# Small gaps between the on-chip buffers of a two-layer transformer kernel

## The chip, the cores and the metric

The kernel runs on one core of one Trainium2 chip. The metric is the device time of one execution, in microseconds (us). Engines are named as in the profile: PE is TensorE's matmul, PEld its weight load (which overlaps the matmul), DVE is VectorE, ACT is ScalarE, POOL is GpSimd, SP is SyncE (it issues DMAs here). SBUF is the on-chip memory that the engines read their operands from; a buffer in it takes the same byte range in each of 128 partitions.

## The reference, cut to what matters

512 frames with 1024 channels each go through two blocks, all in float32.

- Block 1: RMS norm, an input projection into 24 tiles of 128 channels, stick-breaking attention, chunked attention with a relative bias, a short convolution, a grouped norm, an output projection; then a gated feed-forward layer (gate and up with 2816 columns each, and down).
- Block 2: RMS norm, an input projection into 42 tiles, a convolution with 31 taps, sliding-window attention with sinks, three further 1024x1024 projections, and a retrieval layer: `q = h @ w_pq`, scores against 2 x 128 sub-keys per head, the 16 best pairs of 8 heads for each frame, and for these experts (of 16384)

```
a   = gelu(einsum("ced,cd->ce", u_emb[idx], h))
out = einsum("ce,ced->cd", gate * a, v_emb[idx])
```

The kernel computes the retrieval densely: every frame against all 16384 rows of `u_emb`, times a table of gates that is zero for the experts that were not chosen, times all of `v_emb`.

## The kernel before, in words

Activations lie transposed, channels on the partitions and 512 frames along the row, so one tile is 128 x 512 float32 (2048 bytes a partition). A float32 product is made from three products of a rounded type, fp32r: each operand is split into a high part (the value rounded by a copy into an fp32r buffer) and a low part (the value less the high part). `three` (L1040) issues high x high (L1042), low activations x high weights (L1043) and high activations x low weights (L1044), each 128x128 weights against 128x512 activations. That is where the lines L1042 to L1044 come from, whatever the stage is.

The weights come in 218 slots of 128 x 2048 float32 (`w_slots`): 90 for the projections, 64 for the table `u`, 64 for the table `v`. Each slot goes through the same pipeline, in two buffers that alternate: SP loads `raw` (L381, L400) when the low part of the slot two before is made; ACT copies `raw` into `wh` (`high`, L531) when PE is through with that buffer; one of DVE (L1640 in the stages with little DVE work, L2208 in the late ones) and POOL (L457, L512) subtracts into `wl`; PE then runs 48 matmuls on the slot (16 pieces of 128x128 weights, three products each). The high and low activations are `hh` and `hl` in most stages, `hidh` and `hidl` in the down projection, `gah` and `gal` for the table `v`, and views `gh`, `gl`, `qh`, `ql`, `z2r`, `csinr` elsewhere. Waits on semaphores alone order the engines (`w_raw`, `w_hi`, `w_lo` or `uv_lo`, `w_used`).

Beside the slots PE does the small matmuls of attention, norms and scores (L1141 to L1345, L1510), in float32 as it stands, and, between pieces of the table `u`, 1024 small float16 matmuls that make the gate table (L1552). DVE does the 31 taps of the convolution (L1910) and the search for the 16 best (`unit`, L2138 to L2184), which runs while PE works on the first slots of the table `u`; the slots after it need its result (L1567).

The memory: `sb` hands out buffers one behind the other, `esb` as well, in stacks that reuse the same space in different stages. Before `hh` stand `cst` (3584 bytes), `vec` (1556 bytes, which the allocator rounds up to 32 bytes) and a few constants. `hh`, `hl`, `xT`, `raw`, `wh` and `wl` have 16384 bytes each, and the buffers behind them (`tmp`, `sqb`, `lnb`, `z1`, `z2`, `hidh`, `ast`, `gah` ...) mostly multiples of 512 bytes. The addresses that follow from that are, for `hh`, 21664, which is 160 modulo 512, and so 160 modulo 512 for `hl`, `xT`, `raw`, `wh`, `wl`, `tmp`, `z1`, `z2`, `hidh`, `hidl`, `gah`, `gal`, `at`, `qT`, `skT` too; `cst` begins at 128 modulo 512, `kdup` at 352.

Of the kernel before, what the change touches and what calls it, by code (L numbers as in the profile page):

```python
# [15 lines left out]
P = 128  # L16
# [162 lines left out]
def build(nc, ins, out):  # L179
    with ExitStack() as ctx:  # L180
        def sb(name, shape, dt=F32):
            return ctx.enter_context(nc.sbuf_tensor(name, shape, dt))
# [14 lines left out]

        ps = ctx.enter_context(nc.psum_tensor("ps", [P, 8, S], F32))
        hh = sb("hh", [P, KD, S], F32R)
        hl = sb("hl", [P, KD, S], F32R)  # L200


        xT = sb("xT", [P, KD, S])
        raw = sb("raw", [P, 2, 2048])
        wh = sb("wh", [P, 2, 2048], F32R)
        wl = sb("wl", [P, 2, 2048], F32R)

        early = ExitStack()

# [2148 lines left out]
```

## Time and profile before

| | us |
|---|---|
| median of 3 runs | 2661.2 |
| lowest, highest | 2659.51, 2662.67 |
| the profiled execution | 2658.19 |
| its span, first to last instruction | 2656.4 |

| engine | busy us | share of the span |
|---|---|---|
| PE | 2619.3 | 99% |
| PEld | 2116.1 | 80% |
| DVE | 1601.4 | 60% |
| ACT | 1028.5 | 39% |
| POOL | 410.3 | 15% |

The mean granted clock of TensorE is 0.998 of full speed. A matmul's end in the trace is modelled, so the duration of one (some 390 ns) overlaps with the next; the distance from one start to the next is what a matmul costs in a dense row of them.

### The profile page before, as it was taken

Reading aid. Unit: us, or ns where it says so; the run is one execution under the profiler, and the core shown is the slowest. Engines: PE = TensorE matmul, PEld = TensorE weight load, DVE = VectorE, ACT = ScalarE, POOL = GpSimd, SP = SyncE. Lnnn points to the kernel's source line nnn. Section 1 sums busy time; section 2 is a strip of 40 time slices with the busy share of each in tenths; the row PEclk is TensorE's granted clock in tenths of the full one; section 3 lists DMA queues with packets and bytes.
Section 4 is the critical chain, followed back from the end, with each engine's and each line's share of the span. In section 5 each row is a group of like instructions: output and inputs, shape, how many; then the busy total and the mean of one; then the engine's idle time right before and its main releaser. Section 6 shows DMA issues by size and latency. Waiting matters only on the chain.

```text
span 2656.4 us, 33800 instructions
## 1 busy us (share of the span) xinstructions
PE 2619.3 (99%) x12616; PEld 2116.1 (80%) x12616; DVE 1601.4 (60%) x2440; ACT 1028.5 (39%) x1334; POOL 410.3 (15%) x147
## 2 busy tenths in 40 slices
PE   8999999999999999999999999999999999999998
PEld 6767888888876778888888888888888888888886
DVE  4467211213999976579998988888344444444444
ACT  4465322214346763232223455555332222222223
POOL 0001455542010003424444000000000000000000
PEclk9999999999999999999999999999999999999999
DMA  5111222222222222223333365465565555555552
GB/s 184 48 48 69 97 102 97 99 95 95 95 84 76 68 80 96 95 95 145 148 142 143 135 230 192 186 233 201 198 229 189 189 189 191 195 197 195 194 196 95
DMA packets 121737, 374.37 MB, mean 141 GB/s; under 512 B 7553, under 2 KB 73217, under 8 KB 92737
## 3 DMA queue, kind: packets, MB, share of 16 engines
q1 hardware_dynamic: 117968, 333.74, 35.5%
q10 hardware_dynamic: 2016, 35.26, 3.4%
q0 software_dynamic: 1680, 4.46, 0.6%
q8 instruction: 39, 0.64, 0.1%
q14 instruction: 34, 0.27, 0.0%
HBM read 301.86 MB, written 69.21 MB: 140 GB/s over the span
## 4 chain that ended last, share of the span: by engine, by line
PE 83%; DVE 13%; issue 2%; ACT 2%; DMA 0%; DVEq 0%; POOL 0%; POOLq 0%; ACTq 0%
PE ps L1042 26%; PE ps L1044 25%; PE ps L1043 25%; PE ps L1552 2%; DVE cand_t L2179 1%; DVE z L1910 1%; DVE cand_t L2175 1%; DVE sel L2181 1%; DVE wl L1640 1%; DVE topi L2141 1%; DVE topi L2151 1%; DVE sc L2144 1%; DVE sel L2184 1%; DVE bpos L2141 1%; DVE bpos L2151 1%
## 5 line engine op out<-in xcount | busy, mean ns | idle before, releaser
L1042 PE MATMUL ps<-hh,wh 128*128 128x512 f32 x1968 | 783.3, 398 | 9.3 <-DVE wl L1646 8.0
L1044 PE MATMUL ps<-hh,wl 128*128 128x512 f32 x1968 | 768.8, 391 | 0.0
L1043 PE MATMUL ps<-hl,wh 128*128 128x512 f32 x1968 | 767.8, 390 | 0.0
L531 ACT ACTIVATE wh<-raw 128x2048 fp32r<-128x2048 f32 x217 | 414.9, 1912 | 771.2 <-PE ps L1044 769.9
L2208 DVE TENSOR_TENSOR wl<-raw,wh 128x2048 fp32r<-128x2048 f32 x101 | 231.3, 2290 | 432.8 <-ACT wh L531 432.8
L1042 PEld LDWEIGHTS ps<-hh,wh 128*128 128x128 f32 x1968 | 370.2, 188 | 98.9 <-issue 15.6
L1044 PEld LDWEIGHTS ps<-hh,wl 128*128 128x128 f32 x1968 | 370.0, 188 | 79.3
L1043 PEld LDWEIGHTS ps<-hl,wh 128*128 128x128 f32 x1968 | 370.7, 188 | 74.3 <-issue 1.0
L1042 PE MATMUL ps<-gah,wh 128*128 128x512 f32 x1024 | 398.7, 389 | 0.0
L1044 PE MATMUL ps<-gah,wl 128*128 128x512 f32 x1024 | 398.7, 389 | 0.0
L1043 PE MATMUL ps<-gal,wh 128*128 128x512 f32 x1024 | 398.7, 389 | 0.0
L457 POOL TENSOR_TENSOR wl<-raw,wh 128x2048 fp32r<-128x2048 f32 x50 | 230.4, 4608 | 637.4 <-ACT wh L531 637.4
L1043 PEld LDWEIGHTS ps<-gal,wh 128*128 128x128 f32 x1024 | 192.2, 188 | 39.9
L1042 PEld LDWEIGHTS ps<-gah,wh 128*128 128x128 f32 x1024 | 192.2, 188 | 39.9
L1044 PEld LDWEIGHTS ps<-gah,wl 128*128 128x128 f32 x1024 | 192.2, 188 | 39.8
L520 POOL TENSOR_TENSOR pf<-pf,at 128x512 f32<-128x512 f32 x3 | 3.7, 1263 | 1185.0 <-ACT at L1029 1185.0
L1910 DVE SCALAR_TENSOR_TENSOR z<-z,vec 128x511 f32<-128x511 f32 (+14 forms) x240 | 163.4, 733 | 0.0
L512 POOL TENSOR_TENSOR wl<-raw,wh 128x2048 fp32r<-128x2048 f32 x27 | 128.2, 4749 | 183.3 <-ACT wh L531 183.3
L952 ACT ACTIVATE ast<-ps 128x512 f32<-128x512 f32 x64 | 38.2, 598 | 242.4 <-PE ps L1044 242.4
L991 ACT ACTIVATE stage<-ps 128x512 f32<-128x512 f32 x128 | 129.4, 1122 | 0.0
L981 ACT ACTIVATE ast<-ps 128x512 f32<-128x512 f32 x64 | 38.2, 598 | 194.8 <-PE ps L1044 194.8
L1640 DVE TENSOR_TENSOR wl<-raw,wh 128x2048 fp32r<-128x2048 f32 x39 | 89.2, 2288 | 21.4 <-ACT wh L531 21.4
(259 smaller groups left out, 3006.8 us busy)
## 6 DMA issues: line engine op xcount, KB each, us to landing
raw<-in_w_slots SPq DMA_DIRECT2D x217, 1024.0 KB, 4.8
a_spill<-ast SPq DMA_DIRECT2D x64, 512.0 KB, 2.6
gate_table<-stage ACTq DMA_DIRECT2D x8, 4096.0 KB, 13.0
at<-a_spill SPq DMA_DIRECT2D x64, 512.0 KB, 5.8
tt<-gate_table SPq DMA_DIRECT2D x64, 512.0 KB, 6.8
lnb<-z POOLq DMA_DIRECT2D x36, 64.0 KB, 1.9
xT<-in_x SPq DMA_DIRECT2D x4, 512.0 KB, 7.2
bt<-in_rel_tiles POOLq DMA_DIRECT2D x1, 2048.0 KB, 12.2
```

The source lines that it names most:

```text
L457: pool.tensor_tensor(wl[:, b, :], raw[:, b, :], wh[:, b, :].bitcast(F32), ALU.subtract).then_inc(sem("w_lo"), 1)
L512: pool.tensor_tensor(wl[:, b, :], raw[:, b, :], wh[:, b, :].bitcast(F32), ALU.subtract).then_inc(sem("uv_lo"), 1)
L531: act.activation(wh[:, b, :], raw[:, b, :], ACT.Copy).then_inc(sem("w_hi"), 1)
L991: act.activation(stage[:, q % 2, :, c:c + 4].rearrange("p e c -> p c e"), ps[:, 2 * j + a, :].rearrange("p (c e) -> p c e", c=4), ACT.Copy ...
L1042: nc.tensor.matmul(bank, whi, xhi, start=start, stop=False)
L1043: nc.tensor.matmul(bank, whi, xlo, start=False, stop=False)
L1044: return nc.tensor.matmul(bank, wlo, xhi, start=False, stop=stop)
L1552: last = nc.tensor.matmul(ps[:, 2 * r + t // 4, NKEYS * (t % 4):NKEYS * (t % 4) + NKEYS], oh[r][:, 0, t, :], oh[r][:, part, t, :], start=( ...
L1640: dve.tensor_tensor(wl[:, g % 2, :], raw[:, g % 2, :], wh[:, g % 2, :].bitcast(F32), ALU.subtract).then_inc(sem("w_lo"), 1)
L1910: dve.scalar_tensor_tensor(acc[:, back:S], u[:, 0:S - back], w, acc[:, back:S], ALU.mult, ALU.add).then_inc(sem("cv2_y" if m == TAPS else ...
L2141: step(dve.max_index(idx[:, a, 0:8], vals[:, a, 0:8], rows[:, a, :]))
L2208: dve.tensor_tensor(wl[:, b, :], raw[:, b, :], wh[:, b, :].bitcast(F32), ALU.subtract).then_inc(sem("uv_lo"), 1)
```

## The change

Four buffers that nothing reads or writes are put between the others: 32 bytes ahead of `hl`, 64 bytes ahead of `wh`, 160 bytes ahead of `wl`, 160 bytes behind `wl`. No instruction is added, removed or moved; only addresses are different.

```diff
         hh = sb("hh", [P, KD, S], F32R)
+        sb("off_hl", [P, 8])
         hl = sb("hl", [P, KD, S], F32R)
-
-
         xT = sb("xT", [P, KD, S])
         raw = sb("raw", [P, 2, 2048])
+        sb("off_wh", [P, 16])
         wh = sb("wh", [P, 2, 2048], F32R)
+        sb("off_wl", [P, 40])
         wl = sb("wl", [P, 2, 2048], F32R)
+        sb("off_rest", [P, 40])
```

Where the buffers then begin, modulo 512 bytes:

| buffer | before | after |
|---|---|---|
| `hh` | 160 | 160 |
| `hl`, `xT`, `raw` | 160 | 192 |
| `wh` | 160 | 256 |
| `wl` | 160 | 416 |
| `tmp` and all buffers behind it that were at 160 | 160 | 64 |
| `kdup` | 352 | 256 |
| `cst` | 128 | 128 |

The last byte in use moves from 228608 to 229024 of the 229376 in a partition.

## Rows read from the trace of the kernel before

**Rows 1.** The page's part 1: busy us, share of the span, instructions.

```profile
PE 2619.3 (99%) x12616; PEld 2116.1 (80%) x12616; DVE 1601.4 (60%) x2440; ACT 1028.5 (39%) x1334; POOL 410.3 (15%) x147
```

**Rows 2.** The page's part 4: the chain that ended last, by engine.

```profile
PE 83%; DVE 13%; issue 2%; ACT 2%; DMA 0%; DVEq 0%; POOL 0%; POOLq 0%; ACTq 0%
```

**Rows 3.** Windows: us, then busy us of PE, PEld, DVE, ACT, POOL; clock, DMA.

```profile
0.00:66.00 66.00, 58.02 (x241) 44.33 (x241) 29.96 (x40) 31.12 (x49) 1.79 (x6) 1.00 0.50 182
...
666.00:866.00 200.00, 188.63 (x938) 144.11 (x937) 191.20 (x352) 102.97 (x230) 15.78 (x32) 1.00 0.26 85
...
2066.00:2266.00 200.00, 200.00 (x884) 165.62 (x883) 84.70 (x73) 54.36 (x38) 0.00 (x0) 1.00 0.57 191
```

**Rows 4.** Timeline of PE and PEld in the table `v`: start us, us, what.

```profile
2199.94 0.39 PE L1042 MATMUL ps<-gah,wh 128*128 128x512 f32 x1
2199.95 0.19 PEld L1043 LDWEIGHTS ps<-gal,wh 128*128 128x128 f32 x1
2200.17 0.39 PE L1043 MATMUL ps<-gal,wh 128*128 128x512 f32 x1
...
2200.40 0.39 PE L1044 MATMUL ps<-gah,wl 128*128 128x512 f32 x1
...
2200.62 0.39 PE L1042 MATMUL ps<-gah,wh 128*128 128x512 f32 x1
...
2205.38 0.39 PE L1042 MATMUL ps<-gah,wh 128*128 128x512 f32 x1
```

**Rows 5.** DMA issues by tile: count, KB each, median us to landing.

```profile
raw<-in_w_slots SPq DMA_DIRECT2D x217, 1024.0 KB, 4.8
```

**Rows 6.** Timeline of PE: float32 matmuls of 512 columns, two each.

```profile
80.06 1.02 PE L1148 MATMUL ps<-sqb,cst 128*128 128x512 f32 x2
...
84.71 1.02 PE L1157 MATMUL ps<-z 64*128 64x512 f32 x2
```

**Rows 7.** One line's instructions: duration ns min/median/max, L1157 in 84.6:85.5.

```profile
L1157 PE MATMUL ps<-z x3: 483/589/589, 84.4 to 85.1; 64*128 64x512 f32 x2, 64*128 64x384 f32 x1
```

**Rows 8.** Groups by line: count, busy us, mean ns, idle before.

```profile
L1044 PEld LDWEIGHTS ps<-hh,wl 128*128 128x128 f32 x1968 | 370.0, 188 | 79.3
...
L1148 PEld LDWEIGHTS ps<-sqb,cst 128*128 128x128 f32 x32 | 5.2, 190 | 1.0 <-issue 0.6
```

**Rows 9.** Single lines, duration ns min/median/max: the fp32r copies and subtractions.

```profile
L531 ACT ACTIVATE wh<-raw x217: 1893/1912/1925, 15.2 to 2621.7; 128x2048 fp32r<-128x2048 f32 x109
L2208 DVE TENSOR_TENSOR wl<-raw,wh x101: 2281/2292/2294, 1473.9 to 2623.7; 128x2048 fp32r<-128x2048 f32 x101
L2251 DVE TENSOR_TENSOR at<-at,tt x128: 683/685/693, 1933.2 to 2616.8; 128x512 f32<-128x512 f32 x128
L457 POOL TENSOR_TENSOR wl<-raw,wh x50: 4596/4605/4631, 248.8 to 1147.7; 128x2048 fp32r<-128x2048 f32 x50
```

**Rows 10.** Groups by form, DVE in 666:1066: the taps, at 4-byte shifts.

```profile
L1910 DVE SCALAR_TENSOR_TENSOR z<-z,vec 128x511 f32<-128x511 f32 x8 | 5.9, 747 | 0.0
...
L1910 DVE SCALAR_TENSOR_TENSOR z<-z,vec 128x504 f32<-128x504 f32 x8 | 5.6, 743 | 0.0
...
L1910 DVE SCALAR_TENSOR_TENSOR z<-z,vec 128x482 f32<-128x482 f32 x8 | 5.4, 715 | 0.0
```

**Rows 11.** Waits, whole span: us in total, times, longest us.

```profile
ACT wh L531 <- PE ps L1044: 769.9, 103, 9.0
POOL wl L457 <- ACT wh L531: 637.4, 50, 216.2
DVE wl L2208 <- ACT wh L531: 432.8, 68, 9.6
```

**Rows 12.** Waits of PE in 1174:1457, the search for the 16 best.

```profile
PE ps L1567 <- DVE sel L2202: 1.3, 1, 1.3
```

**Rows 13.** Windows, 1174:1457: busy us of PE, PEld, DVE, ACT, POOL; clock, DMA.

```profile
1174.00:1457.00 283.00, 281.71 (x1284) 234.62 (x1284) 255.46 (x869) 83.86 (x90) 114.50 (x24) 1.00 0.37 137
```

**Rows 14.** One line's instructions: the product of the search, beside POOL's subtractions.

```profile
L2179 DVE TENSOR_TENSOR cand_t<-cand_t,topf x16: 1224/1226/5406, 1197.3 to 1447.1; 128x1024 f32<-128x1024 f32 x16
```

**Rows 15.** Timeline: PE where it starts again after a pause.

```profile
1458.44 0.39 PE L1043 MATMUL ps<-hl,wh 128*128 128x512 f32 x1
1458.67 0.39 PE L1044 MATMUL ps<-hh,wl 128*128 128x512 f32 x1
...
1459.59 0.39 PE L1042 MATMUL ps<-hh,wh 128*128 128x512 f32 x1
```

## The prediction

> **What bounds the kernel now.** I read the busy shares first, then the chain of waits, then the windows, then the start times of single matmuls, since a change of addresses can only act through how long single instructions take. PE is busy for 2619.3 of 2656.4 us [rows 1], and the chain that ended last is PE for 83% and DVE for 13% [rows 2]. The windows say where the rest is: the first 66 us have 8 us without PE, the stage of the convolution (666:866) 11.4 us, and the late stages none: 2066:2266 has PE busy for all 200 us [rows 3]. So the reader is to see a kernel whose end moves with the pace of PE over about 2370 us, and with DVE in three short stretches.
>
> The pace: in the table `v` the L1042 matmuls at 2199.94 and 2205.38 are 24 matmuls apart, so one costs 5.44 / 24 = 226.7 ns [rows 4]. The 217 equal loads and one that is split make 218 slots [rows 5], at 48 matmuls each that is 10464 matmuls of this form; 10464 x 226.7 ns = 2372 us, 89% of the span. At full clock (2.4 GHz; the windows show 1.00 [rows 3]) 512 columns at one a cycle would be 213.3 ns, so each matmul has 13.3 ns more than its columns, 139 us in all. This is the only place in the trace with something large that a change of addresses might give back, if those 13.3 ns are two reads of SBUF in each other's way.
>
> **The change, part by part.** Nothing is issued more or less; the counts of instructions, waits, DMAs and bytes stay. Each part is an address.
>
> *PE's two streams (`hh`/`hl` or `gah`/`gal` against `wh`/`wl`).* Before, both begin at 160 modulo 512; after, they are apart by 64 to 352 bytes. Does the pace depend on that? Three readings say no.
> First, the trace has pairs of both sorts. L1157 reads `z1` against `z1`, both at 160; L1148 reads `sqb` (160) against `cst` (128). Two float32 matmuls of 512 columns take 1.02 us with the one and 1.02 us with the other [rows 6]. A single one is drawn 589 ns long [rows 7], so the second starts 430 ns behind the first in both.
> Second, the weight load takes 188 ns where both operands are at 160 and 190 ns where the weights are at 128 [rows 8]. A load that was held up by equal places would be the longer one.
> Third, the streams do not stay in step. In one matmul the activations go over 2048 bytes in some 213 ns and the weights over 512 bytes in 188 ns [rows 4, 8]. Their distance therefore grows by about 1500 bytes during each matmul and passes every place modulo 512 about three times; what a fixed distance of 64 to 352 bytes changes is when a meeting falls, not how many there are. Only if the length of a meeting depended on its moment would the sum change.
> The bounds: below, half of the 430 ns of a float32 matmul of 512 columns, which goes over its columns twice (430 / 2 = 215 ns, the nearest row of a matmul without the extra; rows 6 and 7), so 10464 x (226.7 - 215) = 122 us less. Above, the widest steady pace that the trace has for this form, just after a pause: from 1458.44 to 1459.59 are 5 matmuls, 230 ns each [rows 15], so 10464 x 3.3 ns = 35 us more. I take 0, nearest to the comparison of equal and unequal pairs, which differ by less than the 10 ns that those rows resolve (1% of 1.02 us); in the dense stages the sum is sensitive to less, 1 ns a matmul being 10.5 us, so both ends stay for the rivals.
>
> On this, the Trainium skill has something for each side. "SBUF — State Buffer", section "Who interferes with whom", gives TensorE two independent read ports, one for the moving operand and one for the weight load, and says that only DVE and GpSimd contend, over one port pair. By it the gaps do nothing; the even pace of rows 4, with DVE 42% and ACT 27% busy beside it, agrees, but no row before shows the two ports being independent.
> "TensorE: Matmul & The Clock Gate", section "Back-to-back issue gap", speaks the other way: it has N / 2.4 + 2.5 ns for a warm matmul, 215.8 ns for 512 columns. The 215 ns of half a float32 matmul agree with it, the 226.7 ns of the fp32r form do not, so some 11 ns would be there to be won. As an estimate from that page, all of it won is 10464 x 10.9 = 114 us, a time near 2547 us; that is the first rival below, whose own time is worked out from rows.
>
> *ACT, DVE and POOL on `raw`, `wh`, `wl`.* With all three at one place, the subtraction takes 2292 ns for 2048 elements and the product of `at` and `tt` 685 ns for 512 [rows 9]. The difference is 1607 ns for 1536 elements, 1.046 ns an element, and leaves 149 ns as a fixed part. Within one line nothing scatters: 2281 to 2294 over 101 executions, POOL's 4596 to 4631 over 50, ACT's 1893 to 1925 over 217 [rows 9], although other engines and DMAs come and go beside them. Nor does a shift matter that is not a multiple of 16 bytes: the taps read 511, 504 and 482 columns, that is from 4, 32 and 120 bytes into the row, at 747, 743 and 715 ns [rows 10]; 29 columns for 32 ns is again 1.1 ns a column. Value 0. The price if I am wrong is covered: ACT waits 769.9 us for PE, POOL 637.4 and DVE's L2208 432.8 us for ACT [rows 11]. A slot is 48 x 0.2267 = 10.9 us of PE, and copy plus POOL's subtraction take 1.9 + 4.6 = 6.5 us of it [rows 9], so each could grow by 4 us before PE waits. Bounds: 0 from both sides in these stages.
>
> *DVE in the stages where it leads.* From 1174 to 1457 the search is 255.5 us of DVE in 283 us [rows 13], and PE then waits 1.3 us for its result [rows 12]. So a faster search gives at most 1.3 us, and a slower one costs all that is over. All its buffers move together (160 to 64), so their distances from each other stay. The convolution's taps read and write `z2` alone and shift likewise. I take 0. Bounds: a gain of 1.3 us in the search and none elsewhere; a loss of 1% of 283 us, 3 us, which is what the scatter of single DVE lines (under 1% [rows 9]) allows.
> The search has one thing that depends on moments: the product L2179 takes 1226 ns alone and up to 5406 ns when it meets a POOL subtraction [rows 14]. One meeting more or less is 4.2 us, of which a gain can use only 1.3. Which ones meet follows from the order of the waits, which does not change; I leave 0 and keep +4 in the range.
>
> *DMAs.* `raw` takes 4.8 us to land [rows 5] against the 10.9 us of a slot, and the chain holds 0% of DMA [rows 2]. Value 0, covered by 6 us a slot.
>
> The sum is 0 from every part: the profiled execution of 2658.19 us stays 2658 us. It lies 3.0 us under the median of the runs shown (2661.2), which themselves spread over 3.2 us. As the change is compared with that median, the time I give is 2661.
>
> **The rivals.**
> *A, PE's extra cycles are meetings of the two streams, and the gaps avoid them.* For it: the extra is 32 cycles for 512 bytes of weights, a round number (one for each 16 bytes), float32 matmuls do not have it, and in every dense stage the buffers stand at one place. Against: the three readings above. Won as a whole the pace is 215 ns and the time 2661 - 122 = 2539 us; won by a tenth, 2649 us. It decides from 0.5 ns a matmul (5.3 us) on.
> *B, the other side: the equal places are what keeps the streams apart, and the gaps bring them together.* Place: the same 10464 matmuls. For it: the load of the next weights starts 10 ns after a matmul does [rows 4], at the same place, an order that may be favourable, and the price is paid everywhere, since PE has no slack in the late windows [rows 3]. Against: the same readings. At the 230 ns of rows 15 the time is 2661 + 35 = 2696 us; it decides from 0.5 ns a matmul on.
> *C, a meeting of DVE and POOL more in the search.* 2661 + 4 = 2665 us, still within what can't be told from no change.
> *D, the gaps do not do what they say* (rounded away, or nothing is read from the shifted buffers): the same time as my forecast. Each gap is a multiple of 32 bytes, so the addresses do move.
>
> **How the numbers follow.** A measurement of this kernel can tell about 0.2%, 5.3 us, from no change. My forecast with C and D has 0.79 and gives 2655.9 to 2666.5 us. Rival A has 0.12, most of it on a part of the 122 us, and that is the chance of faster. Rival B has 0.09 and gives slower, most of it under 20 us. The range leaves out about half of A and of B: down to 2650 us (1 ns a matmul), up to 2670 us (0.9 ns a matmul).
>
> **What would show it.** The distance between matmuls in the table `v`, 226.7 ns as in rows 4, decides nearly everything: 215 is A, over 227.2 is B, and anything between is their share. The weight load would keep 188 ns; the lines of rows 9 would keep their medians within 10 ns; PE's wait for the search would stay at 1 to 6 us; 2066:2266 would again have 884 matmuls. I am wrong if the pace differs by over 0.5 ns in any dense stage, or if one line of ACT, DVE or POOL becomes longer by so much that PE waits for `wl`.

## The result, and the profile after

The changed kernel takes 2695.0 us (median of 4 runs, 2693.82 to 2695.26) against 2660.5 us of the kernel before: ratio 1.013, 95% interval 1.0114 to 1.0146. It is slower by 34.5 us; 2661 us was forecast, with 2650 to 2670 as the range, so the time lies 25 us outside it. The profiled execution took 2695.26 us with a span of 2693.5 us, 37.1 us over that of before.

Part 1 of the page of the changed kernel, and the chain that ended last [rows 1, 2]:

```profile
PE 2659.4 (99%) x12616; PEld 2118.1 (79%) x12616; DVE 1597.3 (59%) x2440; ACT 1029.3 (38%) x1334; POOL 411.8 (15%) x147
...
PE 93%; DVE 3%; ACT 2%; issue 1%; DMA 0%; POOL 0%; POOLq 0%; SPq 0%; DVEq 0%; ACTq 0%
```

PE has 40.1 us more, the other engines nothing that matters (DVE 4 us less), with the same counts. The chain has lost most of its DVE: 13% before, 3% now.

The windows [rows 3], with the number of instructions in brackets behind each engine's busy time:

```profile
0.00:66.00 66.00, 58.17 (x239) 44.12 (x240) 29.98 (x40) 30.26 (x46) 1.79 (x6) 1.00 0.49 176
...
2066.00:2266.00 200.00, 200.00 (x875) 164.10 (x874) 84.30 (x73) 53.78 (x38) 0.00 (x0) 1.00 0.56 189
```

The first 66 us are as before. In the table `v` PE is busy for all 200 us in both kernels, at the same clock, and gets through 875 matmuls instead of 884. A full row of 9s in the busy digits can hide a slower PE; the count in the window doesn't.

Timeline of PE in the table `v` [rows 4]; all lines behind the change have numbers higher by 2, so L1044 to L1046 are the old L1042 to L1044:

```profile
2299.96 0.39 PE L1044 MATMUL ps<-gah,wh 128*128 128x512 f32 x1
...
2302.71 0.39 PE L1044 MATMUL ps<-gah,wh 128*128 128x512 f32 x1
```

The two are 12 matmuls apart: 2.75 / 12 = 229 ns, where it was 226.7. Over all 1023 trios of that stage which follow each other the starts give 687 ns a trio (high x high, low x high, high x low: 226, 229 and 232 ns to the next start) against 680. On `hh` and `hl` it is worse: 697.7 ns on average over the 1693 trios without other work between (median 699: 235, 230, 232), against 682.0. That average is a mixture: 1117 of these trios take 698 to 700 ns and 576 take 690 to 695, with the same places. On `hidh`, `qh`, `z2r` and `gh` it is 687 as on `gah`.

That accounts for the change: 15.7 ns x 1968 + 6.7 ns x 1024 + 6.6 ns x 496 = 41 us of PE, of which 37 arrive at the end. Part of the rest was hidden in PE's pauses: idle time of PE in the span is 37.1 us before (2656.4 - 2619.3) and 34.1 us after (2693.5 - 2659.4). PE's wait of 1.3 us for the search [rows 12] is gone: a slower PE is now the later of the two.

The lines of the other engines [rows 9], duration ns min/median/max:

```profile
L533 ACT ACTIVATE wh<-raw x217: 1893/1916/1936, 15.3 to 2658.6; 128x2048 fp32r<-128x2048 f32 x109
L2210 DVE TENSOR_TENSOR wl<-raw,wh x101: 2281/2291/2294, 1495.1 to 2660.6; 128x2048 fp32r<-128x2048 f32 x101
L2253 DVE TENSOR_TENSOR at<-at,tt x128: 681/683/693, 1963.0 to 2653.5; 128x512 f32<-128x512 f32 x128
L459 POOL TENSOR_TENSOR wl<-raw,wh x50: 4578/4614/4656, 250.9 to 1163.2; 128x2048 fp32r<-128x2048 f32 x50
```

Medians moved by 4, -1, -2 and 9 ns, 0.3% at most, though `raw`, `wh`, `wl` and `at` now stand at four places instead of one. Only PE minds.

### The profile page after: what moved, and what is told of

Its sections match the earlier page's. It is cut to its first block, busy times and chain, and to the rows that moved or that the text cites. A ratio compares the mean times of both kernels' runs of the same rounds, so it can differ in the third digit from the quotient of the medians.

```text
span 2693.5 us, 33800 instructions
## 1 busy us (share of the span) xinstructions
PE 2659.4 (99%) x12616; PEld 2118.1 (79%) x12616; DVE 1597.3 (59%) x2440; ACT 1029.3 (38%) x1334; POOL 411.8 (15%) x147
## 4 chain that ended last, share of the span: by engine, by line
PE 93%; DVE 3%; ACT 2%; issue 1%; DMA 0%; POOL 0%; POOLq 0%; SPq 0%; DVEq 0%; ACTq 0%
PE ps L1044 29%; PE ps L1046 29%; PE ps L1045 28%; PE ps L1554 2%; DVE z L1912 1%; DVE wl L1642 1%; PE ps L1150 0%; PE ps L1512 0%; PE ps L1218 0%; ACT wh L533 0%; PE ps L1323 0%; PE ps L1229 0%; PE ps L1347 0%; PE ps L1334 0%; PE ps L1245 0%
## 5 line engine op out<-in xcount | busy, mean ns | idle before, releaser
L1044 PE MATMUL ps<-hh,wh 128*128 128x512 f32 x1968 | 798.1, 406 | 8.5 <-DVE wl L1648 7.7
L1046 PE MATMUL ps<-hh,wl 128*128 128x512 f32 x1968 | 778.8, 396 | 0.0
L2210 DVE TENSOR_TENSOR wl<-raw,wh 128x2048 fp32r<-128x2048 f32 x101 | 231.2, 2289 | 440.5 <-ACT wh L533 440.5
L1044 PEld LDWEIGHTS ps<-hh,wh 128*128 128x128 f32 x1968 | 370.2, 188 | 103.2 <-issue 15.6
L1046 PEld LDWEIGHTS ps<-hh,wl 128*128 128x128 f32 x1968 | 370.4, 188 | 92.5
L1046 PE MATMUL ps<-gah,wl 128*128 128x512 f32 x1024 | 403.5, 394 | 0.0
L1044 PE MATMUL ps<-gah,wh 128*128 128x512 f32 x1024 | 397.3, 388 | 0.0
L1044 PEld LDWEIGHTS ps<-gah,wh 128*128 128x128 f32 x1024 | 192.2, 188 | 43.0
L1046 PEld LDWEIGHTS ps<-gah,wl 128*128 128x128 f32 x1024 | 192.5, 188 | 38.2
L2224 DVE TENSOR_TENSOR same<-iota_t,slot_t 128x1024 f16<-128x1024 f16 x64 | 78.2, 1221 | 46.4 <-PE ps L1554 46.3
```

The source lines that it names most:

```text
L1044: nc.tensor.matmul(bank, whi, xhi, start=start, stop=False)
L1046: return nc.tensor.matmul(bank, wlo, xhi, start=False, stop=stop)
L2210: dve.tensor_tensor(wl[:, b, :], raw[:, b, :], wh[:, b, :].bitcast(F32), ALU.subtract).then_inc(sem("uv_lo"), 1)
L2224: dve.tensor_tensor(same[:, :, :], iota_rows, slots(0), ALU.is_equal).then_inc(sem("oh_part"), 1)
```

## The experiments

A single run of an unchanged kernel scatters over some 5 us (the kernel before, in all runs here: 2658.2 to 2662.8), so times are given beside the run of the kernel before on the same chip, and the verdicts rest on the distances between matmuls. "Distance" is the place of the weights less that of the activations, modulo 256 bytes.

### PE alone, one distance at a time (m1_pairs)

```diff
+SETTINGS += [(0, 16 * i) for i in range(64)]
+for n, (m, w) in enumerate(SETTINGS):
+    for r in range(24):
+        nc.tensor.matmul(ps[:, n % 8, :], wt[:, w // 4:w // 4 + P], mv[:, m // 4:m // 4 + S], ...)
```

> Leaves out the whole computation: one fp32r weight tile and one activation row are loaded, and PE alone runs rows of 24 matmuls of 128x512, each row with its own distance between the bytes of the activations and of the weights; nothing else runs beside. Theory S (streams): the cost of an fp32r matmul depends on the distance, modulo 512 bytes or a part of it, between the activations that it reads and the weights that are loaded meanwhile; 226.7 ns at distance 0, as in the kernel before, and values from 216 to 235 ns elsewhere, with period 512. Theory N (neighbours): the pace is lost to reads and writes of DVE, ACT, POOL or DMAs beside PE; then all distances show one pace, at or under 226.7 ns. Theory A (address): it hangs on where a single operand begins; then rows in which both are shifted alike differ from distance 0.

Timeline of PE; each row is 25 matmuls, from the first start to the last end, so (time - 0.39) / 24 is the pace. The rows are distances 0, 32, 96, 192 and 256:

```profile
16.78 5.83 PE L64 MATMUL ps<-mv,wt 128*128 128x512 f32 x25
...
33.10 5.99 PE L64 MATMUL ps<-mv,wt 128*128 128x512 f32 x25
...
55.45 6.00 PE L64 MATMUL ps<-mv,wt 128*128 128x512 f32 x25
...
88.97 5.89 PE L64 MATMUL ps<-mv,wt 128*128 128x512 f32 x25
...
111.12 5.83 PE L64 MATMUL ps<-mv,wt 128*128 128x512 f32 x25
```

The paces from the starts alone, in ns:

```
distance      0     16     32     48     64     80     96    112    128    144    160    176    192    208    224    240
pace      226.7  226.7  233.4  233.3  233.2  232.1  234.3  233.3  233.5  233.5  233.1  230.0  228.9  233.3  233.4  226.8
```

The same 16 values came back over 1024 bytes, within 0.2 ns, and with 96 bytes plus each whole kilobyte up to 6. With activations moved instead of weights the values are those of the negative distance within 0.8 ns. So Theory S holds, but for its period, which is 256 bytes and not 512, and for its lower end: nothing is under 226.7. With nothing beside PE, Theory N falls. Rows with both shifted alike average 226.9 to 227.8 ns, but the excess is in the first seven intervals of a row (224 to 236 ns), where the addresses have just changed; from there on they have 226.7 ns like the rest. So an address by itself is worth nothing here, and what ran before is felt for some matmuls.

### The same in the full kernel (e_shift_all, e_w256b, e_w96b)

```diff
+        sb("off_all", [P, 24])     # e_shift_all: all distances stay 0
         hh = sb("hh", [P, KD, S], F32R)
...
+        sb("off_wh", [P, 64])      # e_w256b: 256 bytes, nothing else
+        sb("off_wh", [P, 24])      # e_w96b: 96 bytes, and 160 behind wl
         wh = sb("wh", [P, 2, 2048], F32R)
```

> The kernel before with one gap of 96 bytes ahead of hh: all buffers of the dense stages begin at 256 modulo 512 instead of 160, their distances from each other stay 0. Theory S: no change, 2660 us, three matmuls in 680 ns. Theory A (an operand at 160 is well placed, one at 256 or 64 is not): slower, between 2665 and 2700 us.

> The kernel before with one gap of 256 bytes ahead of wh: raw and the activations hh, hl at 160 modulo 512, wh, wl and all behind at 416. Theory S with a period of 256 bytes, as in the rows of matmuls: no change, 2658 to 2664 us, three matmuls in 680 ns. With a period of 512 in the full kernel, or if any gap between them costs: the stages on hh slower, over 2675 us.

> The kernel before with one gap of 96 bytes ahead of wh and one of 160 behind wl: wh and wl 96 bytes past the activations modulo 256 in every stage, all the rest at equal places modulo 256. The row of matmuls at distance 96 took 234.3 ns each against 226.7 at distance 0. Theory S: three matmuls in about 700 ns instead of 680, 3488 trios, 60 to 80 us more, about 2720 to 2740 us: worse than the changed kernel, though the gaps are smaller. Theory M (it is having many different distances, not one, that costs): less than the changed kernel's loss, under 2695 us.

| | us | before, same chip | trio on `hh`, ns | trio on `gah`, ns |
|---|---|---|---|---|
| e_shift_all | 2662.7 | 2661.5 | 682.0 | 680.0 |
| e_w256b | 2663.2 | 2659.9 | 682.0 | 680.0 |
| e_w96b | 2726.6 | 2659.9 | 702.9 | 702.9 |

The window 266:466 (on `hh`) of the kernel before, then the windows 266:466 and 2066:2266 (on `gah`) of the kernel with a distance of 96 bytes everywhere:

```profile
266.00:466.00 200.00, 200.00 (x882) 165.25 (x881) 44.00 (x61) 59.95 (x63) 102.93 (x34) 1.00 0.27 97
...
266.00:466.00 200.00, 200.00 (x854) 160.48 (x853) 45.29 (x62) 59.05 (x61) 97.23 (x33) 1.00 0.27 95
2066.00:2266.00 200.00, 200.00 (x855) 160.80 (x854) 80.92 (x70) 51.51 (x36) 0.00 (x0) 1.00 0.55 188
```

3 x 234.3 = 702.9 ns from the row of matmuls is the trio in the full kernel to the tenth. A distance of 96 bytes in every stage costs 67 us, nearly twice the change itself; a gap of 256 bytes, larger than any of the change, costs nothing that can be measured (3 us, 0.13%). Theories A and M fall, and with them a period of 512 bytes.

The profile shows where even the 3 us arise. In e_shift_all and e_w256b the window 666:866, the stage of the convolution, has a granted clock of 0.97 and 914 matmuls, where the profiled kernel before has 1.00 and 938; in 866:2466 they have 7923 and 7922 against its 7919. Both have a mean granted clock of 0.996, as have the runs of the kernel before that took 2661.5 and 2662.8 us; with 0.998 it took 2658.2 and 2659.9. So a difference of 2 to 5 us between single runs can be the clock and not the addresses.

### Is it the buffers behind wl? (e_rest_back, e_rest160)

```diff
-        sb("off_rest", [P, 40])
+        sb("off_rest", [P, 64])    # e_rest_back, from the changed kernel
...
+        sb("off_rest", [P, 40])    # e_rest160, from the kernel before, the only gap
```

> The changed kernel with the last gap 96 bytes larger, so that all buffers behind wl stand at 160 modulo 512 again; hh 160, hl 192, wh 256, wl 416 as in the changed kernel. Theory S: the stages on gah, hidh, qh, z2r and gh now have nearly the distances of hh (96 and 256), and their three matmuls go from 687 to about 694 to 698 ns; 1520 trios by 8 to 11 ns are 12 to 17 us more, 2707 to 2712 us; the stages on hh keep 697 ns. Theory R (the place of the buffers behind wl, for DVE and ACT, costs the time): back towards 2660 us. Theory A: gah and the others at 160 return to 680 ns, 2684 us.

> Only the last gap: tmp and all behind it 160 bytes further; hh, hl, xT, raw, wh, wl at equal places. Map theory: the stages on hh keep 680 ns; in the 1520 others (gah, hidh, qh, z2r, gh) the weights are 96 past the activations modulo 256, (0, 96, 96) is 702.8 ns; 22.8 x 1520 = 35 us, about 2694 us. Part theory, or DVE and ACT being the ones that lose: another pattern, with ACT's or DVE's medians longer by over 1%, or under 2672 us.

e_rest_back: 2699.2 us (before 2661.5); trios 697.4 ns on `hh`, 690.0 on `gah`. Putting those buffers back where they had been made it 3 to 4 us slower still (37.7 us over the kernel before, where the change has 34.5), since `gah` at 160 is now 96 from `wh`; Theories R and A fall. The 690 is less than the 694 to 698 expected, and the time 2699 less than 2707. e_rest160, the windows as above:

```profile
266.00:466.00 200.00, 200.00 (x880) 164.93 (x879) 44.27 (x61) 59.20 (x62) 102.89 (x34) 1.00 0.27 98
2066.00:2266.00 200.00, 200.00 (x855) 160.78 (x854) 82.39 (x72) 49.17 (x35) 0.00 (x0) 1.00 0.56 189
```

880 in the first window against 882 before, 855 against 884 in the second: the loss sits in just the stages whose activations were moved, 702.9 ns a trio. 2696.3 us (before 2662.8) against the 2694 expected.

### The other gaps one by one (e_hl32, e_wh64, e_wl160)

```diff
+        sb("off_hl", [P, 8])       # e_hl32; 224 bytes behind hl bring the rest back
         hl = sb("hl", [P, KD, S], F32R)
...
+        sb("off_wh", [P, 16])      # e_wh64; 192 bytes behind wh
+        sb("off_wl", [P, 40])      # e_wl160; 96 bytes behind wl
```

> Only the first gap: hl 32 bytes further, all the rest at equal places modulo 256. Map theory: the trio map of PE alone has 696 ns for (low activations 32, weights 0, 0) against 680, on the 1968 trios of hh and hl; 16 ns x 1968 = 31 us, about 2690 us, and 680 ns in the table v. Part theory (each gap gives its share of the 34.5 us of the whole change): a third of it or less, under 2672 us.

> Only the second gap: wh 64 bytes further, all the rest at equal places modulo 256. Map theory: (0, 64, 0) is 700 ns against 680, on all 3488 trios; 20 ns x 3488 = 70 us, less some 5 that DVE hides, about 2725 us, twice the loss of the whole change. Part theory: under 2695 us.

> Only the third gap: wl 160 bytes further, all the rest at equal places modulo 256. Map theory: (0, 0, 160) is 700 ns, about 2725 us as with wh alone. Part theory: under 2695 us.

| only this gap | us (before 2662.8) | trio on `hh`, ns | trio on `gah`, ns |
|---|---|---|---|
| hl by 32 | 2684.4 | 697.5 | 680.0 |
| wh by 64 | 2704.6 | 696.8 | 693.3 |
| wl by 160 | 2719.3 | 700.0 | 700.0 |
| rest by 160 | 2696.3 | 681.8 | 702.9 |

The losses are 21.5, 41.8, 56.4 and 33.5 us, 153 us together, for a change that costs 34.5 with all four. (The run of before beside them had a mean granted clock of 0.996, like the last of the four; the others had 0.997, 0.998 and 0.998, so by the runs of before at either clock their losses may be some 2 to 5 us too small.) So the gaps have no shares of their own: what counts is the set of distances that they leave. The map's 696 and 700 ns for hl and wl come back in the kernel (697.5; 700.0), the 700 for wh does not: 697 and 693, and 2705 us instead of 2725. On `hidh`, where the places differ by the same 64 bytes as on `gah`, the same run has 700.0 ns: three paces for one set of distances. For hl the time is 6 us under the one expected although the trio is as mapped: PE is busy for 30 us more than in the profile of before (2649.5 us), but its span is only 26 us longer (2682.6 us), so 4 us went into PE's pauses, and the run of before beside it was 2 us above the one that the expectation started from.

### Which type, which size (m2b_kinds)

```diff
+SETTINGS += [("r", 512, 128, d), ("f", 512, 128, d), ("h", 512, 128, d)]   # fp32r, float32, float16
+SETTINGS += [("r", 448, 128, d), ("r", 384, 128, d), ("r", 512, 96, d), ("r", 512, 64, d), ("r", 512, 32, d)]
```

> Leaves out the whole computation: rows of 24 matmuls of PE alone, of three types (fp32r, float32, float16), at distances 0, 96, 192 and 32 bytes, and fp32r with fewer columns of activations or of weights. Theory S2: only fp32r, which reads 4 bytes a column at one column a cycle, has no room for the reads of the weights, so float32 (about 430 ns) and float16 (about 216 ns) show the same at all distances, within 1 ns; and the extra of fp32r over its columns (13.3 ns at distance 0, 21 at 96) falls with the columns of the weights, to about a half at 64. Rival: all types hang on the distance alike, float32 by some 7 ns at 96; then float32 was a good stand-in and the comparison in the prediction only met a lucky distance. Rival 2: the extra falls with the columns of activations and not with the weights (a slower stream, no meetings).

Each float32 matmul is two instructions in the trace (192 records for 96 matmuls). Timeline: float32 at distances 0 and 96 (18 instructions each, an end 0.59 us behind its start), then float16 at 96 (23 instructions, 0.38 us):

```profile
29.87 7.89 PE L74 MATMUL ps<-xT,raw 128*128 128x512 f32 x18
...
61.28 7.89 PE L74 MATMUL ps<-xT,raw 128*128 128x512 f32 x18
...
50.47 5.13 PE L74 MATMUL ps<-m,w 128*128 128x512 f16 x23
```

| cycles (2.4 GHz) over the columns | distance 0 | 32 | 96 | 192 |
|---|---|---|---|---|
| fp32r | 32.0 | 47.4 | 50.3 | 37.4 |
| float32, one of its two instructions, over 2 x 512 | 6.0 | 6.0 | 5.9 | 5.9 |
| float16 | 5.9 | 6.1 | 5.9 | 6.1 |
| fp32r, 448 / 384 columns | 37.9 / 32.0 | | 32.0 / 32.0 | |
| fp32r, weights 96 / 64 / 32 wide | 39.8 / 41.1 / 44.1 | | 41.9 / 32.1 / 41.1 | |

The row for 448 and 384 columns is taken from the ninth matmul on: the row of 384 columns at distance 0 begins with seven intervals of 171 to 185 ns behind the row of another length, and then has 173.3 ns throughout.

The first half of S2 holds: float32 and float16 have 6 cycles over their columns at all four distances, only fp32r minds. The second half falls, and so does its rival 2: the extra does not fall steadily with the weights (128, 96, 64 and 32 wide: 32, 40, 41, 44 at distance 0 and 50, 42, 32, 41 at 96) nor with the columns. No form shows less than 32 cycles, and there are 0 to 18 more. What is best for one length is not for another: with 448 columns distance 96 is the better one (200.0 against 202.5 ns), with 384 both settle at 173.3 ns.

### Is there a better place? (m3b_trios, m4_fine)

```diff
+SETTINGS += [(32 * a, 32 * b, 32 * c) for b in range(8) for c in range(8) for a in range(8)]
+for r in range(8):      # three matmuls: (wh, mv), (wh, mv + xl), (wl, mv)
```

> Leaves out the whole computation: PE alone runs 8 trios (high x high, low x high, high x low) in each of 512 settings of the places of the low activations, high weights and low weights in steps of 32 bytes modulo 256, the high activations at 0. Additive theory: a trio costs the sum of its three distances from the first map, so 680 ns where all are equal and nothing below it; the changed kernel's distances (hl 32, wh 96, wl 0 modulo 256 from hh) give 702 less a few ns. Rival: the places act together, and some setting is under 680 ns (by 5 ns or more); then a kernel at that setting would be 17 us or more faster than the kernel before.

> Leaves out the whole computation: the trio map again, at 500 of the places that are odd multiples of 16 bytes in one coordinate at least, in random order, then three settings of the first map each twice in a row behind equal places. Floor theory: 32 cycles over the columns are the least that an fp32r matmul of this length shows, so no setting is under 680 ns, and the kernel before stands at the best placement. Rival: between the 32-byte steps there is a setting under 680 ns, by 2 ns or more, worth 7 us or more in the full kernel. History: a setting behind equal places gives the same as in the first map within 1 ns if only the places count; if the order that PE comes from counts too, (0, 64, 0) can give 693 instead of 700, as in the table v of the kernel with that gap.

Timeline of PE in the first map, 24 matmuls each, (time - 0.39) / 23 x 3 is a trio: equal places, then the changed kernel's (32, 96, 0), then its place for `gah`, (0, 192, 96):

```profile
17.66 5.60 PE L66 MATMUL ps<-mv,wt 128*128 128x512 f32 x24
...
1097.63 5.73 PE L66 MATMUL ps<-mv,wt 128*128 128x512 f32 x24
...
2295.72 5.66 PE L66 MATMUL ps<-mv,wt 128*128 128x512 f32 x24
```

From the starts they are 680.0, 696.7 and 687.5 ns; the full kernel has 697.7 and 687 (the first as the mixture of about 694 and 700 named above, so that its nearness to 696.7 is in part chance). Of 512 settings, equal places are at 680, the best of the others at 684.2, (160, 0, 128), the mean at 696, the worst at 708. The sum of three single distances meets the mean of all trios but hardly tells one from another: it misses by 6 ns (standard deviation), 20 at most, while the trios themselves scatter by 4.4, and the correlation is 0.1. The places act together. In the second map, of 500 settings in between, three come to 680.3 to 680.5 ns although their places are far apart, such as (160, 240, 128); the next is 686.3, none is under 680. Sixteen bytes on one operand can cost what 32 do: (240, 0, 0) has 686.7. So among the 1012 of 4096 settings that were tried none is a version that would beat the kernel before by its places: it stands at the lowest pace seen, 3 x 544 cycles.

The second map also repeated settings behind equal places. (0, 64, 0) gave 700 and (32, 0, 0) 696 as in the first, but (32, 96, 0) gave 700.2 twice where the first map had 696.7:

```profile
2849.46 5.76 PE L69 MATMUL ps<-mv,wt 128*128 128x512 f32 x24
```

The rest can't be the places modulo 256. Equal places always came back to 226.7 ns a matmul, within eight intervals, behind four different settings. Elsewhere PE seems to fall into one of several rhythms for the same places: 694 or 700 ns on `hh` in the changed kernel, 693.3, 696.8 or 700.0 ns in e_wh64. What picks the rhythm is not shown; that it is what PE comes from is a guess, since no run here sets it on purpose.

## Why the prediction was wrong

**The step that failed** is the value 0 for "PE's two streams". The runs show that this pace depends on the distance between activations and weights modulo 256 bytes: 226.7 ns at distance 0 and 228.9 to 234.3 ns at distances of 32 to 224 bytes, with PE alone. All else held: ACT, DVE and POOL within 0.3%, DMAs as before, the search never more than a wait of 1.3 us (now none), and the sensitivity of 10.5 us a nanosecond: the trios on `hh`, `gah` and the rest give 3.9 ns a matmul on average (231.0 against 227.1), 41 us of PE, of which 37 reach the end of the span. One small reading was off without effect: the scatter of single DVE lines is not under 1%, L2251 has 683 to 693 ns [rows 9], 1.5%.

**The first reading** [rows 6, 7] took float32 matmuls as a stand-in. m2b_kinds shows that an instruction of float32 spends two cycles on a column and has 6 over at all four distances: it is blind to what fp32r minds. It also shows two records for each float32 matmul, so the 1.02 us are the two instructions of one matmul, not two matmuls, and the 215 ns of the lower bound are half of one instruction. The pair was a fair comparison of places and a wrong one of types; no fp32r pair with unequal places was in the trace, and 0 "nearest to the row" was nearest to the wrong row.

**The second reading** (the weight load takes 188 ns at equal places) is true after the change too, 188 to 189 ns, while the matmul behind it starts up to 8 ns later. A load's duration doesn't show what the matmul beside it loses. The pair of 188 and 190 ns was also one of types, an fp32r load against a float32 load.

**The third reading** (the streams slide past each other, so a fixed distance can't change the sum) was an argument without a row, and m1_pairs refutes it: the sum over a matmul hangs on where they begin, with a step of 7 ns from a distance of 16 bytes to one of 32. It assumed that each meeting costs the same; the prediction named the condition under which it would fail ("Only if the length of a meeting depended on its moment") and gave it no price. Whether there are such meetings at all is not shown, only what the distance costs.

**Rival A** (the extra 13.3 ns are meetings that gaps avoid) is refuted for the placements tried: no fewer than 32 cycles remain in over 1000 of them, in shorter matmuls and with narrower weights, and none is better than `before`. What these 32 are stays open.

**Rival B** named the place and the direction: equal places are the good ones, and the gaps undo that, on the 10464 matmuls. Its 2696 us lie 1 us from the result, but by luck: the 230 ns came from a restart after a pause [rows 15], while the changed kernel has a mixture of 226 to 235 ns whose mean is 231.0, and the 41 us of PE that this makes lose some on the way to the end. It deserved far more than 0.09. What spoke for it was in the text: a pace of exactly 544 cycles looks like a rhythm in step, and what is in step can be put out of step; no run shows that this is what happens inside PE. A range of 20 us around an unmeasured effect that costs 10.5 us a nanosecond was too narrow.

The Trainium skill's page "SBUF — State Buffer", section "Who interferes with whom", gives TensorE two independent read ports and names the pair of DVE and GpSimd as the only contention. In these runs PE alone loses up to 8 ns a matmul by where its own two operands begin, so for fp32r the measurement decides against it, as far as independent ports mean that the pace does not depend on the two places; it does not show where in PE or SBUF the time goes. The formula of "TensorE: Matmul & The Clock Gate", section "Back-to-back issue gap", N / 2.4 + 2.5 = 215.8 ns, is met by float16 to 0.1 ns at all four distances, and by fp32r at none (226.7 at best). The section gives it as the gap of an isolated matmul and has some 131 ns for a sustained stream of 512 columns; the prediction left that out, and no run here comes near it: the float16 rows, each matmul with its weight load, ran at 215.8 ns.

## What to carry to other kernels

Where PE runs fp32r matmuls of 512 columns back to back, let activations and weights begin at exactly the same place modulo 256 bytes. A few bytes off already cost: 4 bytes 6 to 10 ns a matmul, and 16 bytes cost nothing in the row with one distance but 6.7 ns in a trio with one operand moved. Buffers whose sizes are multiples of 256 bytes keep equal places by themselves, and small buffers of another size allocated between them cost 0.8 to 2.5% here. Judge a dense stage by the matmuls that it gets through in a window, not by PE's busy share, and measure a disputed cost with the very type that the kernel uses. When several edits act through one resource, undoing one of them tells little: here each gap alone cost between 62% and 163% of the whole. And leave out the first matmuls of a test row: the row before is still felt in them.

## What the runs showed of the hardware that was not expected

- fp32r, 128 weights by 512 columns, PE alone: 544 cycles at equal places modulo 256 bytes, up to 562 elsewhere in steps of 16 bytes; an instruction of float32 or float16 has 6 cycles over its cycles for the columns at all four distances tried.
- The effect goes by the difference of the two places and repeats every 256 bytes; steps of 4 bytes count too: from equal places, activations 4 bytes further give 236.8 ns, weights 4 bytes further 232.4 ns.
- Which distance is good depends on the length: at 448 columns 96 bytes is 2.5 ns better than 0, at 384 columns the same, at 512 columns 7.6 ns worse.
- The same places can give several paces: 696.7 and 700.2 ns a trio with PE alone, 694 and 700 in turn on `hh` in the changed kernel. At equal places, a change of places or of length just before is felt for up to eight intervals.
